# Prompt mixers: the near part of the hierarchical scores in 64-wide blocks with one far level, in place of 32-wide blocks with two

## What is computed

```python
def hgrn_scan(q, k, v, lf, S0):
    def step(S, inp):
        qc, kc, vc, lfc = inp
        G = jnp.cumsum(lfc, axis=1)
        diff = jnp.where(incl[None, :, :, None, None], G[:, :, None] - G[:, None, :], -jnp.inf)
        attn = jnp.einsum('bthk,bshk,btshk->bhts', qc, kc, jnp.exp(diff))
        o = jnp.einsum('bthk,bhkv->bthv', qc * jnp.exp(G), S) + jnp.einsum('bhts,bshv->bthv', attn, vc)
        Gl = G[:, -1]
        S_new = jnp.exp(Gl)[..., None] * S + jnp.einsum('bshk,bshv->bhkv', kc * jnp.exp(Gl[:, None] - G), vc)
        return S_new, o
```

## Time and profile before

| what | value |
|---|---|
| time, median of 3 executions | 3874.49 us (3873.87 to 3901.2) |
| the profiled execution: time, span | 3883.73 us, 3881.9 us |
| mean granted clock of TensorE in it | 0.906 |
| busy in the span: PE, weight loads, DVE, ACT, POOL | 3382.0, 3081.4, 1906.4, 1353.4, 431.0 us |
| instructions | 55383, of them 22914 matmuls and as many weight loads |
| instruction fetch, queue q8 | 190 packets, 3.11 MB |
| window 1044 to 1935 us (end of tile 0 to the tail) | 891 us, PE busy 711.80, DVE 626.36, ACT 284.06, POOL 364.26 |

### The profile page before, as it was taken

One profiled execution on the slowest core, in us unless ns is written; L12 is line 12 of the kernel. 1 busy time (PEld: TensorE's weight loads), 2 busy tenths in 40 slices (PEclk: granted clock), 3 DMA queues, 4 the chain that ended last, 5 costly groups with the idle time before them and its releaser, 6 DMA issues. The chain is left out here.

```text
span 3881.9 us, 55383 instructions
## 1 busy us (share of the span) xinstructions
PE 3382.0 (87%) x22914; PEld 3081.4 (79%) x22914; DVE 1906.4 (49%) x2538; ACT 1353.4 (35%) x2084; POOL 431.0 (11%) x450
## 2 busy tenths in 40 slices
PE   4999999994578778778835996999999999999998
PEld 3899999993467767777734876999999999999987
DVE  6233322221476676666644673445444454454465
ACT  6234323320233333332211553334333343343354
POOL 0000000000444444444230000000000000000000
PEclk6999999997787787877856998999999999999999
DMA  4222233215312212212023556434434334334353
GB/s 182 63 59 59 62 83 92 71 57 201 110 55 69 82 53 72 83 42 82 18 60 114 200 191 235 153 119 177 147 131 179 141 131 179 142 140 158 136 201 114
DMA packets 233036, 450.44 MB, mean 116 GB/s; under 512 B 42028, under 2 KB 115938, under 8 KB 228674
## 3 DMA queue, kind: packets, MB, share of 16 engines
q1 hardware_dynamic: 230666, 428.34, 32.6%
q10 hardware_dynamic: 2128, 18.56, 1.2%
HBM read 363.38 MB, written 83.47 MB: 115 GB/s over the span
## 5 line engine op out<-in xcount | busy, mean ns | idle before, releaser
L2721 PE MATMUL ff_p<-ff_h_hi,ff_w_hi 128*128 128x384 f32 (+1 forms) x1536 | 502.4, 327 | 23.9 <-DMA ff_h_lo<-tmp_h 23.9
L2723 PE MATMUL ff_p<-ff_h_hi,ff_w_lo 128*128 128x384 f32 (+1 forms) x1536 | 502.6, 327 | 0.0
L2722 PE MATMUL ff_p<-ff_h_lo,ff_w_hi 128*128 128x384 f32 (+1 forms) x1536 | 501.8, 327 | 0.0
L412 PE MATMUL pin_pz<-hi,pin_whi 128*128 128x424 f32 (+1 forms) x1320 | 469.0, 355 | 13.9 <-DVE pin_wlo L528 13.9
L414 PE MATMUL pin_pz<-hi,pin_wlo 128*128 128x424 f32 (+1 forms) x1320 | 466.8, 354 | 0.0
L413 PE MATMUL pin_pz<-lo,pin_whi 128*128 128x424 f32 (+1 forms) x1320 | 466.8, 354 | 0.0
L2740 PE MATMUL ff_p<-ff_w_lo,ff_f_hi 128*128 128x512 f32 (+1 forms) x1088 | 426.7, 392 | 0.0
L2741 PE MATMUL ff_p<-ff_w_hi,ff_f_lo 128*128 128x512 f32 (+1 forms) x1088 | 426.4, 392 | 0.0
L2739 PE MATMUL ff_p<-ff_w_hi,ff_f_hi 128*128 128x512 f32 (+1 forms) x1088 | 423.9, 390 | 0.0
L2824 DVE TENSOR_TENSOR ff_w_lo<-ff_w,ff_w_hi 128x1024 fp32r<-128x1024 f32 x192 | 235.1, 1225 | 345.2 <-ACT ff_w_hi L2772 345.2
L2772 ACT ACTIVATE ff_w_hi<-ff_w 128x1024 fp32r<-128x1024 f32 x192 | 203.6, 1060 | 388.8 <-PE ff_p L2741 384.4
(11 more groups left out here) (504 smaller groups left out, 5720.2 us busy)
## 6 DMA issues: line engine op xcount, KB each, us to landing
ff_w<-in_w_unit SPq DMA_DIRECT2D x192, 512.0 KB, 5.5
ff_w<-in_w_unit SPq DMA_DIRECT2D x48, 2048.0 KB, 8.0
tmp_z<-pin_z SPq DMA_DIRECT2D x32, 1024.0 KB, 5.2
mix_rb<-tmp_rows_p SPq DMA_DIRECT2D x16, 1152.0 KB, 8.7
pin_w<-in_w_in SPq DMA_DIRECT2D x33, 512.0 KB, 8.1
gat_wa<-in_w_ada ACTq DMA_DIRECT2D x8, 2048.0 KB, 22.8
mix_zb<-tmp_z SPq DMA_DIRECT2D x16, 640.0 KB, 4.2
tmp_h<-op_h_hi SPq DMA_DIRECT2D x17, 512.0 KB, 4.2
```

The lines of the kernel that those rows point to most:

```text
L412: pe.matmul(pz[:, g, 0:n], whi[:, u, k], hi[:, k, at:at + n], start=(k == 0), stop=False)
L2721: pe.matmul(dst, w1_hi[:, u, k], hi, start=(k == 0), stop=False)
L2722: pe.matmul(dst, w1_hi[:, u, k], lo, start=False, stop=False)
L2723: mm = pe.matmul(dst, w1_lo[:, u, k], hi, start=False, stop=(k == KT - 1))
```

## The change

Blocks of 64 in place of 32: CB = 64, NEAR = 7. The near part is now the diagonal and levels 0 to 5, two blocks of 64 x 64 for two heads: 28 matmuls per group. Only level 6 is far: two matmuls of 64 x 64 per group, written behind the near columns of the group's own bank (columns 448 to 511), so pc now holds far blocks too. far_scores is gone. The masks and the near sum run over 7 x 64 columns per head, `ph` and `near` grow with them. ACT copies one far block from pc and one from pd, and two diagonal blocks instead of four. state_queries, which overwrites pc, now waits for "far_read" (ACT's far copies) instead of "masked" (DVE's mask of pc). "round" is still raised once per group, now in scores.

```diff
-CB = 1 << BLOCKY
-NEAR = BLOCKY + 1
+CB = P // 2
+NEAR = LEVELS
...
-        near_at = lambda j: 0
-        far32_at = lambda j: NEAR * CB + j * CB
-        far64_at = lambda j: NEAR * CB + 2 * CB + j * HD
+        FAR = slice(NEAR * CB, (NEAR + 1) * CB)
...
                     pe.wait_ge(S("gs"), b(1, 1))
-                    pe.wait_ge(S("masked"), b(2, 1))
+                    pe.wait_ge(S("far_read"), b(1, 1))
...
-                                mm = pe.matmul(dst[at, par, n * CB:(n + 1) * CB], a, q, start=True, stop=True)
-                    return mm
-
-                def far_scores(dst):
-                    for j in range(2):
-                        for s in (0, 2 * CB):
-                            for par in range(2):
-                                pe.matmul(dst[s:s + CB, par, far32_at(j):far32_at(j) + CB], hk[half(par), BLOCKY, j, s:s + CB],
-                                          hq[half(par), BLOCKY, j, s + CB:s + 2 * CB], start=True, stop=True)
-                        for par in range(2):
-                            mm = pe.matmul(dst[half(0), par, far64_at(j):far64_at(j) + HD], hk[half(par), BLOCKY + 1, j, half(0)],
-                                           hq[half(par), BLOCKY + 1, j, half(1)], start=True, stop=True)
-                    return mm
+                                pe.matmul(dst[at, par, n * CB:(n + 1) * CB], a, q, start=True, stop=True)
+                    for par in range(2):
+                        mm = pe.matmul(dst[half(0), par, FAR], hk[half(par), LEVELS - 1, j, half(0)],
+                                       hq[half(par), LEVELS - 1, j, half(1)], start=True, stop=True)
+                    mm.then_inc(S("round"), 1)
...
-                    scores(pc, 0).then_inc(S("round"), 1)
+                    scores(pc, 0)
...
                     scores(pd, 1)
-                    far_scores(pd).then_inc(S("round"), 1)
...
-                    for j in range(2):
-                        for s in (0, 2 * CB):
-                            act.activation(ps[s:s + CB, j:HH:2, s + CB:s + 2 * CB], pd[s:s + CB, :, far32_at(j):far32_at(j) + CB],
-                                           ACT.Copy)
-                        ins = act.activation(ps[half(0), j:HH:2, half(1)], pd[half(0), :, far64_at(j):far64_at(j) + HD], ACT.Copy)
+                    for j, src in enumerate((pc, pd)):
+                        ins = act.activation(ps[half(0), j:HH:2, half(1)], src[half(0), :, FAR], ACT.Copy)
                     ins.then_inc(S("far_read"), 1)
```

## The result

| | before | after |
|---|---|---|
| median of 4 executions | 3874.18 us | 3821.27 us (3819.32 to 3842.47) |
| ratio | 1 | 0.9858, 95% interval 0.9823 to 0.9893 |
| profiled execution: time, span | 3883.73, 3881.9 us | 3823.01, 3821.1 us |
| mean granted clock | 0.906 | 0.916 |

The changed kernel is 53 us faster by the medians, 1.4%. The forecast was 3877 us, with 3848 as the lower end of the range; it was wrong. Between the two profiled executions the difference is 60.8 us. The stretch between the `lt` at 1056.26 us of the earlier trace rows and the one 14 tiles on fell from 818.4 to 755.3 us, so all of that (and 2 us more) lies in the full tiles of the prompt mixers.

A forecast was written before the change was run, and what follows sets the result against it. No engine saturated: a PE, DVE and POOL relay sets tile time, with PE short of instructions at boundaries. -27.5 + 6.5 + 2.2 + 19.0 + 1.0 + 1.2 = +2.4 us on the 3874.5 median gave 3877 us, range 3848 to 3900.

The forecast's parts named there:

- the scores on PE: Score matmuls per tile, 108 to 60: same time in pd, pc's extra 0.6 to 0.7 us hidden; zero.
- the longer near sum: DVE's near sum grows 1.7 us, so L2242 misses POOL's second gap: +19.0 at full clock, +1.0 at half.
- the tile that gets the full clock: Tiles that start at full clock once their wait is gone pay 1.3 us back: five tiles, +6.5 us.
- the jump waits: PE's five waits before kk behind the loop's jump back: buffer starts empty, so their 15.3 us stay.
- Instruction waits: PE out of instructions around the scores: 16.0 us before L1913 and 11.5 before kk go, -27.5 us.
- Rival C: Loop body stays in PE's buffer, so jump waits go too, -15.3 us: 3878 or 3849 us; chance 0.11 together.
- case G: PE's scores bound by number of records, at 12 ns each: pd 1.1 us shorter in 16 tiles, -17, 3860; chance 0.05.
- case A: The summed forecast itself, with L2242 missing POOL's second gap: +2.4 us, 3877 us; chance 0.33.
- The last section of the prediction: Wrong above all if a shifted L2249 changes the order in which DVE and POOL get SBUF mid-tile; unpriced.
- mask 1.1 us: DVE's mask reads 896 elements for 384, +0.55 us; pd's sets the end, +0.22 in ten tiles, +2.2 us.
- state_queries' new wait: It waits for ACT's copies, starting up to 1.0 us later; free but in the tail, some +1.2 us.
- pc's scores hidden behind `attn`: pc's scores take 0.6 to 0.7 us more, covered by PE's wait for `attn`; without that cover, +10 us.

The follow-up runs named there:

- the records put back: Changed kernel with 24 matmuls of each score group made a second time, so a tile again has 108 score matmuls, 64 wide: 3877.08 us, ratio 0.9984.
- the edges moved: Kernel before with 32 tiny matmuls ahead of PE's first tile, shifting instruction packet edges by half a packet against the loop: 3876.44 us, ratio 0.999.
- the short sum: Changed kernel with the near sum over one of its seven levels only, good for timing only: 3848.19 us, ratio 0.9914.

## Why the prediction was wrong

Three terms of the sum failed: the scores on PE, put at zero; the longer near sum with the tile that gets the full clock, put at +20 and +6.5; and the jump waits, which were to stay as they were. The first two are why the gain was missed.

**Instruction waits: mechanism right, jump waits mis-sized.** The reading of "issue" as PE out of instructions held: the waits inside a pass went to zero, came back with the count, and stayed when the loop of before was written out. The -27.5 us came true. The 15.3 us of jump waits, which were to stay, became 26.8 (5.4 each for 3.1), so that the net was -16 us. Why they grew stays open. During a jump wait of after two instruction packets are on q8, during one of before a single one (DMA view, 1318.8 to 1324.3 us of after, then 1226.5 to 1229.9 of before):

```profile
q8 instruction: 2, 0.03, 3.9%
```

```profile
q8 instruction: 1, 0.02, 2.6%
```

The two start within 0.6 us of each other and take 1.1 to 2.1 us each, and PE goes on 3.7 to 4.4 us behind them; behind the single one it went on after 2.5 to 3.1 us. The vanished wait in the scores, which might have covered part of the jump's, does not account for it: with the records put back there is such a wait ahead of all five, and they are still 4.5 to 4.9 us; with the edges moved there is none ahead, and they are 3.1 to 4.5. Rival C, a body that stays in PE's buffer, did not come: PE still fetched 9 packets in a pass (1330 to 1440 us):

```profile
q8 instruction: 9, 0.15, 0.7%
```

By the 128 KB and the 256 instructions in a line of 16 KB that the Trainium skill gives (Advanced Engine Details and Errata, ISA Cache), an estimate is that 2048 instructions are kept; for this body of about 1,760 matmuls and loads (881 and 881 from 1330 to 1440 us) the trace does not bear that out. The same list has only two lines, 512 instructions by the same estimate, and that the trace does not contradict.

**The scores on PE: mis-sized term.** A corner is the part of PE's array that one such small matmul uses. I took 0.11 us per 64-wide record on one corner from the four L1923 records. The changed trace has 48 in 0.88 us, (0.88 - 0.22) / 47 = 14 ns apart, so 56 ns on each of four corners. The 0.11 us stood at the start of a group: there the second record of a corner comes 0.11 us behind the first in the changed trace too, and each later one 0.058; it is no rate. The 32-wide records had been 12 ns apart on eight corners, so a record costs 12 to 14 ns at either width, and the number of records decides: case G, to which I had given 0.05. The sum had 0 for this. Pd went from 1.92 to 1.15 us, -0.66 us from mask to mask (3.53 to 2.87 in a tile at full clock without a wait), some -10 us in all. The direction is that of the Trainium skill (TensorEngine Tiling (Array Packing), Instruction Overhead), which I had set aside on the strength of one row; its some 16 us were an over-estimate.

**What a vanished wait gives back, and the longer sum: wrong sign.** The near sum came out at 3.27 us for a forecast 3.2, L2242 did miss POOL's second gap, and `x` came 1.8 us later in the full-clock tiles (7.8 us behind `lt` for 6.04), just as case A had it. Even in `lt` to `x` the price was only +5.1 us for +20: the four tiles that had the full clock before pay 1.8 each, but the ones that start faster only now had `x` 8.2 us behind `lt`, and now have it at 7.8 to 7.9. Of the 14 tiles six now start at full clock, three at 0.71 to 0.73 and five at half. Above all I ended the calculation at `x`, and took the 1.3 us by which a full-clock tile was longer for a price of the clock itself. In the tile at 1056.26 it was the collision of a decay with hk (gs, 3.99 us; cm in the tile at 1404.63), with PE at half clock behind it, and the 1.8 us shift ended the collision. The last section of the prediction names this order as what could make it wrong, and puts no price on it; the price stood in the trace of before, as part of the 40.7 us that PE waited for L2220. Worth: 22 us by the short sum, where the forecast had +20. That a slower PE makes POOL late is read from the traces and was not tried alone; that the collision costs the time, and that the length of the sum decides whether it happens, the runs show.

**Half clock.** Pc mask to pd mask lost 32.7 us: 16.0 of waits, 9 of cheaper scores, and some 7 because PE no longer comes to `wx` and the scores at half clock in the tiles where PE had been idle earlier. The forecast had no term for this, and none for `yt` to the pc mask (-6.1). I put both down to the idle times that went; no run tried it alone.

**Held as forecast:** mask 1.1 us; `lt` 1.0 us behind the mask; state_queries' new wait (11.4 us of PE in 11 tiles) shows, and costs nothing on the way to `x`, which DVE sets; pc's scores hidden behind `attn` (0.9 us of wait still left).

## What to carry to other kernels

Count PE's records in a burst, not only their columns: here a burst of very short matmuls paid in its own issue time (1.92 us for 1.15), and again when the instruction fetch could not follow (42.7 us of waits for 26.8), and half-clock stretches came behind. When a step on the path gets longer or shorter, follow it past the next instruction to the next place where two engines want the same thing; there the order, not the length, sets the time. A row's rate should be read in the middle of a long run of its kind, not off the first pair.

## What the runs showed of the hardware

A 64 x 64 fp32 record and a 64 x 32 one cost much the same, 14 and 12 ns, in a stream over four and eight corners. A jump back of PE's queue over a body of 1,760 or 2,130 matmuls and loads refetches it each pass (9 and 10 packets) and costs 2.5 to 5.5 us at the jump; the changed kernel written out saves 32 us in five jumps. The engines with short lists fetched nothing from the loop's second pass on. A two-input product of 195 columns on DVE, 0.35 us alone, took 4.11 beside a POOL product of 4.27. And a DVE reduce of 1792 elements into 256 takes 3.27 us, while 256 elements into 256 (one per output) take 0.41: the prediction's fit, 4.9 ns per output, meets the first and not the second.
